# Query blocks with a bank each, late ones in two banks in turn, and small loads on ScalarE's queue, in a two-layer decoder trunk

## What is computed

```python
def sliding_window_attention(h, w_qkv, b_qkv, w_o, b_o, sinks, rel_bias):
    qkv = h @ w_qkv + b_qkv                       # 512 x 1024 @ 1024 x 1280
    q, k, v = split(qkv)                          # 16, 2, 2 heads of 64
    q = q * 64 ** -0.5
    for block n of 128 queries:                   # keys of blocks n-1 and n
        s = q_n @ k.T + bias[bucket(distance)]    # masked to a window of 128
        m = max(max(s), sink)
        p = exp(s - m) / (sum(exp(s - m)) + exp(sink - m))
        o_n = p @ v
    return o @ w_o + b_o
h = x + sliding_window_attention(rms_norm(x, g0), ...)
h = h + hierarchical_moe(rms_norm(h, g1), ...)    # then conv, moe, final norm
```

## Time and profile before

| | us |
|---|---|
| median of 3 runs | 1391.74 |
| lowest and highest | 1391.66, 1393.09 |
| the profiled execution | 1391.13 |
| its span, first to last instruction | 1389.3 |

### The profile page before, as it was taken

The page is one execution under the profiler, slowest core; times in us unless marked ns, Lnnn a source line. Parts: engine busy times, 40 slices in busy tenths (PEclk is TensorE's granted clock), DMA queues, the critical chain, the costliest instruction groups (busy, mean ns, idle before and its releaser), DMA issues.

```text
span 1389.3 us, 15380 instructions
## 1 busy us (share of the span) xinstructions
PE 1256.3 (90%) x6054; PEld 666.7 (48%) x6054; DVE 410.3 (30%) x877; ACT 325.4 (23%) x620; POOL 152.8 (11%) x125
## 2 busy tenths in 40 slices
PE   7989999999999988997399989999999999998881
PEld 5766664444443333432288868744444344333330
DVE  6565551121111111111645552411121111111115
ACT  3247721221122111110421121221121111111112
POOL 5750030000001000001000001100010000000000
PEclk9999999999999999999599999999999999999996
DMA  9200749999999999999713330599999999999995
GB/s 363 82 0 1 303 184 419 429 426 428 428 428 428 427 429 428 428 427 402 243 22 109 123 153 24 240 427 427 427 428 428 429 427 428 428 428 427 428 418 210
DMA packets 65939, 456.17 MB, mean 328 GB/s; under 512 B 16932, under 2 KB 32318, under 8 KB 41316
## 3 DMA queue, kind: packets, MB, share of 16 engines
q1 hardware_dynamic: 53476, 444.29, 76.7%
q0 software_dynamic: 5120, 8.41, 1.6%
q10 hardware_dynamic: 7296, 2.81, 0.8%
HBM read 444.96 MB, written 18.90 MB: 334 GB/s over the span
## 4 chain that ended last, share of the span: by engine, by line
PE 63%; DMA 28%; DVE 7%; ACT 1%; issue 1%; SPq 0%; POOLq 0%; DVEq 0%; ACTq 0%
PE ps L1100 20%; PE ps L872 19%; PE ps L1118 11%; DMA xt<-in_moe_w_gate_up_dram 10%; DMA big<-in_moe_w_gate_up_dram 10%; PE ps L1077 6%; DMA xt<-in_moe_w_down_dram 5%; PE ps L1090 1%; DMA big<-in_attn_w_qkv_dram 1%; PE ps L1109 1%; PE ps L1014 1%; PE ps L1085 1%; PE ps L954 1%; DVE xr L1239 1%; DVE big_parts L1301 1%
## 5 line engine op out<-in xcount | busy, mean ns | idle before, releaser
L1100 PE MATMUL ps<-big,arena 128*64 128x512 f32 x1024 | 228.3, 594 | 21.4 <-DMA big<-in_moe_w_gate_up_dram 20.6
L1509 DVE TENSOR_TENSOR gain<-arena,ps 64x512 f32<-64x512 f32 x64 | 68.6, 1072 | 436.0 <-ACT arena L747 436.0
L747 ACT ACTIVATE arena<-ps 64x512 f32<-64x512 f32 x64 | 37.7, 590 | 521.8 <-PE ps L1100 521.8
L535 POOL DMA_INDIRECT rows<-arena x64 | 62.4, 975 | 861.3 <-DVE arena L1535 833.3
L1100 PEld LDWEIGHTS ps<-big,arena 128*64 128x64 f32 x1024 | 72.4, 137 | 171.5 <-issue 136.4
L1100 PE MATMUL ps<-small,arena 128*64 128x512 f32 x512 | 115.0, 594 | 13.1 <-DMA small<-in_moe_w_gate_up_dram 13.1
L872 PE MATMUL ps<-xt_parts,small_parts 128*128 128x512 f32 x288 | 112.0, 397 | 8.8 <-DVE big L1314 5.8
L1118 PE MATMUL ps<-big,arena 128*64 128x512 f32 x512 | 116.9, 598 | 0.0
L872 PE MATMUL ps<-xr_parts,small_parts 128*128 128x512 f32 x272 | 107.1, 394 | 0.0
L872 PE MATMUL ps<-xt_parts,big_parts 128*128 128x512 f32 x256 | 100.9, 394 | 0.0
L1100 PEld LDWEIGHTS ps<-small,arena 128*64 128x64 f32 x512 | 36.0, 137 | 89.2 <-issue 67.0
(11 more groups left out here) (173 smaller groups left out, 1488.2 us busy)
## 6 DMA issues: line engine op xcount, KB each, us to landing
big<-in_moe_w_gate_up_dram SPq DMA_DIRECT2D x64, 2048.0 KB, 30.3
small<-in_moe_w_gate_up_dram SPq DMA_DIRECT2D x32, 2048.0 KB, 32.1
big<-in_moe_w_down_dram SPq DMA_DIRECT2D x32, 2048.0 KB, 34.2
xt<-in_moe_w_gate_up_dram SPq DMA_DIRECT2D x16, 2048.0 KB, 31.2
arena<-in_moe_w_gate_up_dram SPq DMA_DIRECT2D x16, 2048.0 KB, 30.9
small<-in_moe_w_down_dram SPq DMA_DIRECT2D x16, 2048.0 KB, 33.2
arena<-in_moe_w_down_dram SPq DMA_DIRECT2D x8, 2048.0 KB, 34.3
xt<-in_moe_w_down_dram SPq DMA_DIRECT2D x8, 2048.0 KB, 36.1
```

The source lines that it names most:

```text
L535: nc.gpsimd.indirect_dma_start(out=rows_dram[l], out_offset=bass.IndirectOffsetOnAxis(ap=where[:, j:j + 1], axis=0), in_=y_rows[:, j, :], ...
L747: nc.scalar.activation(silu[BLOCK:P, j, :], ps[2 + j][0:BLOCK, :], ACT.Silu).then_inc(S.silu_ready, 1)
L1100: mm = nc.tensor.matmul(ps[2 + j][half * BLOCK:(half + 1) * BLOCK, :], xg[:, k, j * BLOCK:(j + 1) * BLOCK], w[:, a, half * FF:(half + 1) * ...
L1509: V.tensor_tensor(hid[BLOCK:P, j, :].rearrange("q (k p) -> q p k", p=P), silu[BLOCK:P, j, :].rearrange("q (p k) -> q p k", p=P), ps[2 + j] ...
```

## The change

The biases and sinks are loaded by ScalarE's queue, behind `rel_bias`, no longer by SP's ahead of the query weights. The useless matmuls behind the transposes fall from three calls to one. Early query block j writes bank j and no longer waits for `qk_ready`; the transposes of the values, behind block 1, wait for it instead. VectorE splits block 1 after it has copied the keys, no longer before. GpSimd starts its own splits when VectorE's first two are done. The late blocks use banks 6 and 7 in turn: blocks 4 and 5 wait for no removal, blocks 6 and 7 for that of the block two before, and the first `att_out`, which writes bank 6, waits until block 6 is out.

```diff
@@ sync
             sp.dma_start(key_value_weights()[0], ...).then_inc(kv_in, 16)
-            sp.dma_start(b_rows[0:DT + 2, :], b_qkv[0].rearrange("(j p) -> j p", p=P)).then_inc(attn_in, 16)
-            sp.dma_start(sink_row, sinks[0:1, :].to_broadcast([P, H])).then_inc(attn_in, 16)
             sp.dma_start(big[:, 0], w_qkv[0, :, 0:H * HD].rearrange("(k p) n -> p k n", p=P)).then_inc(query_in, 16)
@@ gpsimd
             pool.wait_ge(query_in, 16)
+            pool.wait_ge(w_split, 2)
             split_query(4)
@@ scalar
             act.dma_start(rel[0:BUCKETS, :], rel_bias).then_inc(rel_in, 16)
+            act.dma_start(b_rows[0:DT + 2, :], b_qkv[0].rearrange("(j p) -> j p", p=P)).then_inc(attn_in, 16)
+            act.dma_start(sink_row, sinks[0:1, :].to_broadcast([P, H])).then_inc(attn_in, 16)
@@ tensor
                     if i == 0:
-                        keep_busy(3, 7)
+                        keep_busy(1, 7)
@@
                 pe.wait_ge(w_split, j + 1)
-                pe.wait_ge(qk_ready, j + 1)
-                queries_of(j, ps[4 + j % 2][:])
+                queries_of(j, ps[j][:])
                 if j == 1:
+                    pe.wait_ge(qk_ready, 2)
                     for t in range(TT):
@@
                 pe.wait_ge(q_split, j - FT + 1)
-                if j > FT:
-                    pe.wait_ge(qk_ready, j + 2)
-                queries_of(j, ps[7][:])
+                if j > FT + 1:
+                    pe.wait_ge(qk_ready, j + 1)
+                queries_of(j, ps[6 + j % 2][:])
@@
             late_queries(7)
+            pe.wait_ge(qk_ready, DT + 1)
             att_out(0)
@@ vector
             split_low(0, *query_weights(0))
-            split_low(1, *query_weights(1))
             dve.wait_ge(qk_ps, 1)
             for g in range(KV):
                 ...
             ins.then_inc(qk_ready, 1)
+            split_low(1, *query_weights(1))
@@
-                take_queries(j, ps[4 + j % 2])
+                take_queries(j, ps[j])
@@
-            take_queries(4, ps[7])
+            take_queries(4, ps[6])
@@
-            take_queries(6, ps[7])
+            take_queries(6, ps[6])
```

## The result

| | before | after |
|---|---|---|
| median of 5 runs each, us | 1391.74 | 1382.43 |
| lowest and highest | 1391.41, 1393.09 | 1381.73, 1386.18 |
| span of the profiled execution | 1389.3 | 1380.0 |

The ratio is 0.9935, with a 95% interval of 0.992 to 0.9949: 9.3 us less. The forecast was 1380.8 with a range of 1379.0 to 1384.0, so the time lies in the range, 1.6 us above the forecast.

What follows compares the result with a forecast made beforehand. It took TensorE (63% of the chain) to bound the kernel, with stalls at banks 4 and 7. Gains of 3.4 + 7.9 - 0.4 = 10.9 us from 1391.13 gave 1380.2, plus 0.6 for the median: 1380.8, range 1379.0 to 1384.0.

Steps and rivals of the forecast that it cites:

- Part 1: Ahead of the keys: two calls of useless matmuls less let the keys start at about 19.1, 1.7 us earlier.
- part 3: Load queues: moving the small loads to ScalarE's queue gains nothing; 0 taken, 0.2 us kept for the range.
- Part 2: Early query blocks: a bank each removes the 1.7 us wait at bank 4; block 0 starts at about 30.2.
- The hold: GpSimd's splits of the query weights, held back from 25.4 to 30.5: priced at nothing.
- Part 4: Late blocks in two banks: the stall ahead of block 6 and its half clock go, 7.9 us in all.
- Rival (b): Between blocks 5 and 7 VectorE becomes the bound through collisions with GpSimd: 1382 to 1384; 10%.
- The clock's charge: At clock returns after idle phases: 0.85 us more at half speed, charged as 0.4 us.
- Rival (a): Under the keys the clock stays low after a 0.4 us gap withholds its rise: 2.0 us lost, 1382.8; 25%.
- Rival (d): Biases land late on ScalarE's queue and hold TensorE's transposes: slower, 3%; milder delay eating 2 to 6 us, 4%.
- Rival (c): At the end the weights' stream absorbs the gain: time within 0.2% of 1391.7; 3%.
- one of the prediction's signs: In the changed kernel, no clock below 1.00 from 25 us until the first MoE is done.
- The first expert load: Layer 0's expert weights: first load expected 11.3 us earlier, near 127.1, with waits for weights as long as before.

Runs made afterwards that it cites:

- e1: Changed kernel with the two small loads (biases, sinks) issued by SP ahead of the query weights again; median 1381.95 us.
- e6: Changed kernel with the two small loads issued by ScalarE after the third tile's square and root instead of behind rel_bias; median 1381.98 us.
- e7: Kernel before with five calls of useless matmuls into bank 6 in the wait ahead of late block 6; median 1391.26 us.
- e4: Kernel before with only a bank for each early query block, the values' transposes waiting for the keys' removal instead; median 1391.11 us.
- e2: Changed kernel with three calls of useless matmuls behind the transposes again instead of one; median 1382.62 us.
- e5: Changed kernel without GpSimd's hold, so it splits as soon as the query weights land; median 1383.21 us.
- e3: Kernel before with only the late blocks in banks 6 and 7 in turn, with their waits; median 1385.60 us.
- e9: e6 with the edit of e8, so later small loads and one useless matmul call moved ahead of the narrow router products; median 1381.12 us.
- e10: e9 with a second closing useless matmul call moved to between the third and fourth tile's narrow router products; median 1384.72 us.
- e11: The changed kernel, unaltered, profiled and timed once more; median 1384.38 us.
- e8: Changed kernel with one closing call of useless matmuls moved ahead of each layer's last narrow router products, four left behind them; median 1383.26 us.

## Why the prediction was right, and where a term was off

**Part 1, 1.7 us forecast, 0.4 measured at the keys, and the half clock under them then cost 0.8.** The keys were put at 19.1 from the last split of x, and that split moved with x itself; the failed step is in part 3, below. With the loads elsewhere (e1, e6) the keys stand at 19.28, so the step itself was right to 0.2 us, for an execution in which the clock falls at the transposes (e7).

**Part 2, 1.7 us, right.** TensorE waits nowhere from the keys to the end of block 3; e4 alone shows 1.80 at the scores, and from the keys to the scores e1 and e2 take 34.27 us where it was 36.13, 1.86 less. What is missing from the forecast place of block 0 is what part 1 lacked. The splits kept their cover: the first is done at 28.2, forecast 27.8 to 30.0.

**The hold, nothing, right** (e5).

**Part 3, "I take 0", the failed step.** It asked only what the two issues cost on ScalarE's own queue, and there the answer held: they took 0.61 and 0.36 us, and ScalarE still stood idle before the first tile of x. It did not ask what the two transfers do to those of x, with which they are now in flight. The price is 1.1 us at the keys (20.38 against 19.28), where 0.2 was kept for the range. The chain of it: the third square waits 0.89 us for its tile and starts at 10.04 instead of 9.04, the last transposes follow at 16.53 instead of 15.36. The sign of the dip stood in the trace of before, between 12 and 13 us, outside any row that the prediction read. The query weights came no earlier: ScalarE's copy of them starts at 25.85, VectorE's first split at 27.0, before at 26.6.

**Part 4, 7.9 us, measured 8.3.** From the scores of unit 2 that precede block 5 to the output product it is 84.37 - 64.91 = 19.46 us; before it ran from 66.41 to 94.15, 27.74. e3 alone gives 8.24, and e7 confirms the 2.0 of the half clock at 1.95. Most of the 0.4 more are the two groups of transposes: the sum takes 0.60 us for each, but the next block starts 0.36 us after them (72.45 to 72.81, 78.36 to 78.72). The slack of 1.2 us at block 7 was 0.6: block 5 is out at 78.1 (77.35 + 0.74 in the row above), block 7 starts at 78.72. Rival (b) had its condition within reach and was not met.

**The clock's charge, 0.4.** At the start of layer 1 the clock came back 5.2 us after L873's first (682.52, up at 687.7), before 3.1: 1.0 us on that chain row (133.25 against 132.29). It did not reach the end, by luck: the execution before had lost 1.1 us right behind it, 72 matmuls in 19.11 us against the 18.00 of the row above. The mechanism was right; the size is a matter of the execution.

**Rival (a)** asked that a gap ahead of the keys withhold the clock, at 2.0 us. Half clock under the keys did occur, at 0.8 us, but not in that way: there was no gap (18.29 + 1.91 is the transposes' start at 20.2), and the clock rose 5.6 us after the last transposes of x began, where before it was 3.8. In e1, e6 and e9 it rose before the useless matmuls ended, so its condition did not arise there either; in e10 and e11 the clock was full through a gap of 1.68 us and fell about 1 us into the keys. In e8 its condition arose: half clock from 17.6, a gap of 1.08 us ahead of the keys at 20.23, and half clock under them until 24.4. From the keys to the scores it took 36.22 us there, 1.95 more than the 34.27 of e1, which is the rival's price; whether the gap or the late fall held the clock down is not shown. **Rival (d)** did not occur: the biases were there (no wait at L884). **Rival (c)** is excluded by the expert wait, as long as before and 9.4 us earlier.

**The sum, against the trace.** At the output product the gain is 94.15 - 84.37 = 9.8 us, of which 8.3 are part 4 and 1.5 all the rest (forecast 3.4). In the router 0.3 went: from the 32 narrow products to the first expert product it was 18.57 us against 18.27, as the clock fell there at 179.1 and had not before. That also answers one of the prediction's signs: it wanted no clock below 1.00 from 25 us until the first mixture of experts is done, and the clock was at half from 179.1 to 182.5. In layer 1 the lead fell from 9.4 to 8.4 at the start, came back to 9.5 by the luck above, and the second router took another 0.4 (9.52 to 9.15), for the same reason. At the end it is 9.3. So the forecast of 10.9 was 1.6 too much: 1.9 too much before the scores, 0.4 too little for part 4, and 0.1 too little for the clock behind it, 0.5 in all where 0.4 was charged.

The first expert load was issued at 128.65 (forecast 127.1), 9.8 us earlier than before.

## What to carry to other kernels

A PSUM bank that is used again by a later block is a wait on the engine that empties it, and where that engine is deep in another queue the wait is long: the second bank for the late blocks alone (e3) gave 6.9 of the 9.3 us. Price a stall with the half clock that follows it (5.1 us of idle time cost 2.0 more). Before moving a small transfer, look at what is in flight at its new place, not only at the queue that issues it; when gains of 1 to 2 us are compared, time the same kernel twice, with the old one beside it, since here that alone moved a median by 2 us, of which the old one shared 1. And before useless matmuls are put into a wait, look at which side of the wait they come to stand: in e8 they stood behind it, and cost 0.93 us a call.

## What the runs showed of the hardware

Two transfers, of 5 and of 8 KB, together left a hole of some 1 us in a stream of about 420 GB/s: 121 to 198 GB/s over 1 us behind x when SP issued them (kernel before, e1, e3, e4, e7), or two neighbouring us of 183 to 270 inside x when ScalarE issued them at 1.7 and 2.4 us (changed kernel, e2, e5, e8, e11). Issued by ScalarE behind the third square (e6, e9, e10) they left none of that size: the window from 12 to 13 us moved 386 to 390 GB/s, and the lowest us behind it 333 to 391.

The granted clock fell to half in all thirteen profiled executions, for 3 to 7 us at a time, at one or more of these places of layer 0: at x's transposes, under the keys, behind the wait for bank 4 or the first scores, in the narrow router products, and behind them. In e11 it fell while TensorE was busy, 1.2 us after a gap of 1.68 us had ended; in e9 0.2 us after the end of a gap of 1.99 us. The narrow products showed it most plainly: 3.66 to 3.73 us for 32 at the full clock, up to 5.42 when it fell among them. The Trainium skill (TensorE: Matmul & The Clock Gate, "What you observe") ties the full clock to sustained matmuls. The traces agree in kind, but two executions of one program differed in where it fell, and no run here explains that.
